# A decoder step with a 32-expert mixture: gate and up weights read with 16 neighbouring rows per partition, and the gathered tokens permuted to match

## The reference, cut to what matters

```python
def hier_moe(xn, p):                  # D_MODEL 2048, 32 experts, MOE_FF 256, float32
    t = xn.reshape(-1, D_MODEL)       # 264 tokens
    ...                               # router: a group of 8 experts, then the 2 best in it
    hg = jnp.einsum('td,edf->tef', t, p['moe_w_gate'])
    hu = jnp.einsum('td,edf->tef', t, p['moe_w_up'])
    hmid = jax.nn.silu(hg) * hu * gates[..., None]
    out = jnp.einsum('tef,efd->td', hmid, p['moe_w_down'])
```

## Time and profile before

| | us |
|---|---|
| median of three runs | 1730.24 (1726.53 to 1732.93) |
| the profiled execution, its own time | 1727.93 |
| its span in the trace | 1725.7 |
| up to the end of `xa_wo` | 1099 |
| router block and the way to the first expert matmul | 1099 to 1154 |
| experts, 16 pairs | 1154 to 1700 |
| final norm and output | 1700 to 1725.7 |

### The profile page before, as it was taken

How to read it: one execution, slowest core, us unless ns; L and a number is a source line. 1 busy time by engine, 2 the same in 40 slices (tenths; PEclk the granted TensorE clock), 3 DMA queues, 4 the chain that set the end, 5 groups by cost and what they waited for, 6 DMA issues and landing times. The chain is left out here.

```text
span 1725.7 us, 20054 instructions
## 1 busy us (share of the span) xinstructions
PE 1571.8 (91%) x7823; PEld 1132.5 (66%) x7823; DVE 675.3 (39%) x1860; ACT 287.2 (17%) x772; POOL 213.9 (12%) x305
## 2 busy tenths in 40 slices
PE   7999989989888788997999699759999999999987
PEld 5888867767677677876886388535545644554445
DVE  3536439999955731001345000332112211321123
ACT  3111101111112321000212000221211211121103
POOL 1110135665610000110000011020000000000000
PEclk9999999999989999998999899879999999999999
DMA  9644433333342566442656956309999999999981
GB/s 282 213 147 144 139 110 110 110 110 110 120 131 86 177 189 199 148 149 96 236 195 248 337 153 243 97 12 367 365 374 373 365 365 378 370 365 364 379 308 51
DMA packets 317993, 376.10 MB, mean 218 GB/s; under 512 B 24931, under 2 KB 289423, under 8 KB 309442
## 3 DMA queue, kind: packets, MB, share of 16 engines
q1 hardware_dynamic: 313242, 370.62, 64.3%
q10 hardware_dynamic: 4664, 4.28, 0.7%
HBM read 363.44 MB, written 11.54 MB: 217 GB/s over the span
## 5 line engine op out<-in xcount | busy, mean ns | idle before, releaser
L917 PE MATMUL ps<-ring,M 128*128 128x256 f32 x1024 | 247.6, 400 | 1.6 <-ACT M L930 1.6
L2342 PE MATMUL ps<-ring,M 128*64 128x512 f32 x1024 | 227.5, 597 | 14.1 <-DMA ring<-in_moe_w_up 13.4
L300 PE MATMUL ps<-X,ring 128*128 128x264 f32 x1024 | 230.1, 388 | 7.5 <-PEq L1497 6.4
L917 PEld LDWEIGHTS ps<-ring,M 128*128 128x128 f32 x1024 | 201.7, 201 | 43.2 <-issue 14.8
L300 PEld LDWEIGHTS ps<-X,ring 128*128 128x128 f32 x1024 | 195.6, 191 | 41.8 <-issue 8.1
L630 PE MATMUL ps<-X,ring 128*128 128x264 f32 x896 | 205.1, 390 | 0.0
L630 PEld LDWEIGHTS ps<-X,ring 128*128 128x128 f32 x896 | 170.8, 192 | 29.4 <-issue 0.4
L2342 PEld LDWEIGHTS ps<-ring,M 128*64 128x64 f32 x1024 | 79.7, 138 | 158.7 <-issue 157.7
L2507 DVE TENSOR_TENSOR M<-M,ps 128x256 f32<-128x256 f32 x16 | 6.7, 421 | 420.2 <-ACT M L2429 420.2
L1795 PE MATMUL ps<-X,ring 128*128 128x264 f32 x512 | 120.0, 392 | 9.4 <-PEq L1549 9.4
L2353 PE MATMUL ps<-SH 128*128 128x264 f32 x512 | 118.2, 389 | 0.7 <-ACT SH L2443 0.7
(11 more groups left out here) (431 smaller groups left out, 1569.0 us busy)
## 6 DMA issues: line engine op xcount, KB each, us to landing
SH<-in_moe_w_down SPq DMA_DIRECT2D x32, 2048.0 KB, 14.7
ring<-in_moe_w_gate SPq DMA_DIRECT2D x64, 1024.0 KB, 11.7
ring<-in_moe_w_up SPq DMA_DIRECT2D x64, 1024.0 KB, 11.9
ring<-in_w_in SPq DMA_DIRECT2D x14, 2048.0 KB, 8.5
ring<-in_xa_wk SPq DMA_DIRECT2D x8, 2048.0 KB, 9.1
ring<-in_xa_wv SPq DMA_DIRECT2D x8, 2048.0 KB, 9.0
ring<-in_w_out SPq DMA_DIRECT2D x8, 2048.0 KB, 8.4
SH<-in_cache_mem_k SPq DMA_DIRECT2D x8, 2048.0 KB, 9.7
```

The source lines that it names most:

```text
L300: mm = nc.tensor.matmul(ps[:, b, 0:T], w[:, k, o * P:(o + 1) * P], xn[:, k, :], start=(k == 0), stop=(k == KB - 1))
L917: mm = nc.tensor.matmul(ps[:, kv_bank(s), a * 256:(a + 1) * 256], memT[:, k, a * P:(a + 1) * P], w[:, k, :], start=(k == 0), stop=(k == KB ...
L2342: mm = nc.tensor.matmul(ps[64 * e:64 * e + 64, 0, :], xg[:, p % 3, k, e, :], gate_up_unit(e, half)[:, :, k % 8, :], start=(k == 0), stop=( ...
```

## The change

The rows of the gate and up weights are split as `(p k)` in place of `(k p)`: partition p gets the 16 neighbouring rows 16p to 16p + 15. A unit takes 8 of these 16, which lie behind one another in memory: a run of 8 KB for each partition in place of 8 runs of 1 KB. The bytes, the buffers and SP's order stay. The matmul's block k then holds the dimensions 16m + k for m from 0 to 127, and no longer 128k + m. So the tokens are put in that order too:

- the prompt tokens when they leave PSUM in the router: the same instructions as before read the bank with a step of 16 numbers, 16 times 32 of them, and write runs of 32 numbers;
- the 8 samples by a new way: 16 transposes in four groups into bank 3, four ScalarE copies that permute them into `xs_tok`, 16 transposes back, and a ScalarE copy into `xsT`, from which GpSimd fills the lists;
- the branch for long lists rebuilds `xn` in the new order by matmuls (it is not taken with these inputs).

```diff
+        def rows_of_expert(name, e):
+            w = I[name][0]
+            return w[e].rearrange("(p k) n -> p k n", k=KB) if isinstance(e, int) else \
+                w[bass.ds(e, 1)].rearrange("o (p k) n -> p (o k) n", k=KB)
...
                     sp.dma_start(gate_up_unit(j % 2, half)[:, w, :, :],
-                                 of_expert(name, e)[:, 8 * half:8 * half + 8, :]).then_inc(unit_loaded[j].sem, 16)
+                                 rows_of_expert(name, e)[:, 8 * half:8 * half + 8, :]).then_inc(unit_loaded[j].sem, 16)
...
         def tok_block(x, n):
-            return x[:, n % 2, 512 * (n // 2):512 * (n // 2) + 512]
+            return x[:, n % 2, :].rearrange("p (k m) -> p k m", k=KB)[:, :, 32 * (n // 2):32 * (n // 2) + 32]
+        def tok_bank(b, rows=P):
+            return ps[0:rows, b, :].rearrange("p (m k) -> p k m", k=KB)
+        xs_tok = work[0:TS, 0:2048].rearrange("p (k m) -> p k m", k=KB)
+        xsT = work[:, 3400:3528].rearrange("p (k b) -> p k b", b=TS)
...
+                for n in range(4):                                   # TensorE, ahead of its wait for chosen_ready
+                    if n:
+                        pe.wait_ge(strow_taken.sem, strow_taken.at(n))
+                    for k in range(4 * n, 4 * n + 4):
+                        mm = nc.tensor.transpose(ps[0:TS, 3, (k % 4) * P:(k % 4 + 1) * P], xn[:, k, TP:T], ident[:, :])
+                    mm.then_inc(strow_done.sem, strow_done.up())
+                pe.wait_ge(strow_taken.sem, strow_taken.at(4))
+                for k in range(KB):
+                    mm = nc.tensor.transpose(ps[:, 3, TS * k:TS * k + TS], xs_tok[:, k, :], ident[0:TS, 0:TS])
+                mm.then_inc(st_done.sem, st_done.up())
...
                 pool.wait_ge(chosen_ready.sem, chosen_ready.at(1))
+                pool.wait_ge(st_taken.sem, st_taken.at(1))
...
-                        gp.tensor_copy(xg[:, b, :, e, CAP:CAP + TS], xn[:, :, TP:T])
+                        gp.tensor_copy(xg[:, b, :, e, CAP:CAP + TS], xsT)
...
-                    nc.scalar.copy(tok_block(x_parts[0], n), ps[:, 4 + n % 4, :]).then_inc(part_ready.sem, part_ready.up())
+                    nc.scalar.copy(tok_block(x_parts[0], n), tok_bank(4 + n % 4)).then_inc(part_ready.sem, part_ready.up())
...
+                for n in range(4):                                   # ScalarE, ahead of the two exponentials
+                    act.wait_ge(strow_done.sem, strow_done.at(n + 1))
+                    nc.scalar.copy(xs_tok[:, :, 32 * n:32 * n + 32], tok_bank(3, TS)).then_inc(
+                        strow_taken.sem, strow_taken.up())
+                act.wait_ge(st_done.sem, st_done.at(1))
+                nc.scalar.copy(xsT.rearrange("p k b -> p (k b)"), ps[:, 3, 0:P]).then_inc(st_taken.sem, st_taken.up())
                 act.wait_ge(r_arg.sem, r_arg.at(1))
                 nc.scalar.activation(rt[:, 0:12], rt[:, 0:12], ACT.Exp).then_inc(r_exp.sem, r_exp.up())
```

More of the change, by code:

```diff
@@ L2046, in build @@
                                             "token_rest_ready", "logit_rows_done", "logit_rows_taken"))
+        strow_done, strow_taken, st_done, st_taken = (signal(f"router_{n}") for n in (
+            "sample_rows_transposed", "sample_rows_taken", "samples_transposed_back", "samples_taken"))
         with nc.Block() as block:
@@ L2138, in _ @@
                     first_part(n)
-                    nc.scalar.copy(tok_block(x_tok, n), ps[:, 4 + n % 4, :]).then_inc(raw_taken.sem, raw_taken.up())
+                    nc.scalar.copy(tok_block(x_tok, n), tok_bank(4 + n % 4)).then_inc(raw_taken.sem, raw_taken.up())
                 for n in range(4, 8):
                     second_part(n)
+                for n in range(4):
[4 more added lines that the diff above has]
+                nc.scalar.copy(xsT.rearrange("p k b -> p (k b)"), ps[:, 3, 0:P]).then_inc(st_taken.sem, st_taken.up())
                 act.wait_ge(r_arg.sem, r_arg.at(1))
@@ L2178, in _ @@
                         dve.wait_ge(part_ready.sem, part_ready.at(n + 1))
-                        tt(tok_block(x_tok, n), ps[:, 4 + n % 4, :], tok_block(x_parts[0], n), ALU.subtract).then_inc(
+                        tt(tok_block(x_tok, n), tok_bank(4 + n % 4), tok_block(x_parts[0], n), ALU.subtract).then_inc(
                             xtok_taken.sem, xtok_taken.up())
@@ L2254, in build @@
         g_silu, g_mid, g_midT = (A[:, 2800 + 256 * i:3056 + 256 * i] for i in range(3))
+        eye_b = H[:, 6144:6208].bitcast(BF16)
+        eye_ready, xn_done, xn_taken = (signal(f"moe_{n}") for n in (
+            "bf16_identity_ready", "tokens_block_rebuilt", "tokens_block_taken"))
         gates_te = gates_tok.rearrange("p a g j -> p a (g j)")
@@ L2275, in _ @@
                 with pe.If(crowd > CAP):
+                    pe.wait_ge(eye_ready.sem, eye_ready.at(1))
+                    for k in range(KB):
+                        if k >= 4:
+                            pe.wait_ge(xn_taken.sem, xn_taken.at(k - 3))
+                        for a in range(2):
+                            for part in range(3):
+                                mm = nc.tensor.matmul(ps[:, 4 + k % 4, a * P:(a + 1) * P],
+                                                      x_parts[part][:, a, k * P:(k + 1) * P], eye_b,
+                                                      start=(part == 0), stop=(part == 2))
+                        mm.then_inc(xn_done.sem, 1)
+                    pe.wait_ge(xn_taken.sem, xn_taken.at(KB + 1))
                     for e in range(EXPERTS):
@@ L2459, in _ @@
                 with dve.If(crowd > CAP):
+                    v.tensor_copy(eye_b, ident[:, :]).then_inc(eye_ready.sem, 1)
+                    for k in range(KB):
+                        dve.wait_ge(xn_done.sem, xn_done.at(k + 1))
+                        v.tensor_copy(xn[:, k, 0:TP], ps[:, 4 + k % 4, 0:TP]).then_inc(xn_taken.sem, 1)
+                    v.tensor_copy(xn[:, :, TP:T], xsT).then_inc(xn_taken.sem, 1)
                     for e in range(EXPERTS):
```

## The result

The changed kernel takes 1715.29 us (median of 4 runs, 1710.92 to 1718.06), the kernel before 1729.82 on the same chip (4 runs, 1726.53 to 1732.93). The ratio is 0.9914 with a 95% interval of 0.9885 to 0.9943: 14.5 us or 0.86% faster. The forecast was 1716 and "faster". Its sum is right to 1 us, yet three of its terms were mis-sized and their errors cancel, which is luck. The traces show this.

What follows compares the result with a forecast made beforehand. Weight transfers were taken to bound the experts' stage by a hair, TensorE next. 1727.93 - 15.1 (loads) + 1.5 (router) = 1714.3, or 1716 us on the median's level; range 1709 to 1730, the forecast case's own 1711 to 1719.

Steps and rivals of the forecast that it cites:

- The bound: Experts' stage: weight transfers set the pace by a hair, 33.96 us a usual pair; TensorE's 33.59 us is next.
- The rate: Gate and up loads: 8 KB runs go at 418 GB/s, cautiously 388, against 348 for 1 KB runs.
- The rivals on the memory's pitch: Gate and up loads: no faster with 8 KB runs, 1732 us (chance 0.08), or slower, 1765 us (0.05).
- The gain in the stage: Experts' stage: all 15 waits on up loads go, 13.4 us plus 1.7 of half-speed clock, 15.1 us gained.
- the wait's price: Experts' stage: TensorE's listed idle time on up loads, 13.4 us in 15 waits, 0.37 in a usual pair.
- The router: Router's last chain: the samples' new copies and transposes make it end 1.5 us later, bounds 0 and 4.
- the slack of 5.2 us: Router: ScalarE has its first exponential at 1127.91 us, VectorE wants it at 1133.13; 6.5 us of work is added.
- a round of four transposes: Router, samples' way: four transposes at 0.12 us each with 0.1 of handover, 0.6 us a round, three rounds.
- The permuted reads: Router: PSUM reads with a step of 16 numbers cost nothing; the rival that they cost, 1724 us, chance 0.13.
- The two rules: Router's PSUM reads: skill rules against non-contiguous access; one gives 0.35 us per 512-column read, some 4 us on the chain.
- The price for small packets: Loads: the skill's fixed 3 cycles a packet lose 8% at 1 KB and 1% at 8 KB, 398 against 430 GB/s.
- The end: Last scatter to the end of the span: no change, 0 us.

Runs made afterwards that it cites:

- the two kernels with a light gather: The kernel before and the changed kernel, each without two of the gather's three bf16 parts: 1724.68 and 1676.23 us, beside 1729.43 for before.
- second trace: The changed kernel run once more, nothing altered, on the same chip as the others, for its trace: 1710.64 us, ratio 0.9898.
- the changed kernel's third trace: The changed kernel unaltered, run beside the kernel without the samples' way on the same chip: 1711.61 us, ratio 0.9909.

## Why the prediction was right

- **The bound.** "The weights set the pace, by a hair" and the next limit, TensorE's own work, hold: the two kernels with a light gather show both sides, and 2 KB and 8 KB loads meet the same limit to 0.01 us.
- **The rate.** Taken as 418 GB/s with 388 as the cautious end. Measured 406 to 442 for 8 KB runs and 388 for 2 KB. The rivals on the memory's pitch fall: half of every 16 KB is read at full rate.
- **The gain in the stage, forecast 15.1, measured 18.3.** The term that was mis-sized is the wait's price. I took the idle time that the waits list (13.4 us) and a pair of 33.59 us, TensorE's busy time. Measured start to start, that is up to the next group, the scatter (line 2353 before, with the row below), the two halves of gate_up take 1264.83 - 1250.40 = 14.43 us before and 1236.35 - 1222.52 = 13.83 after. The wait thus cost 0.60 us where the list says 0.37; the matmuls run into one another, and the modelled end of the last one ahead of a gap, and the refilling after it, count as busy; this is my reading of why, and no run tests it. The difference itself is there in all 15 pairs, 0.22 us each, 3.3 us in all. The last pair has it too: its gate_up took 20.48 us start to start and takes 13.86, that is 6.6 for the 4.70 + 1.69 of the sum. Added up start to start, the 15 pairs before lose 18.4 us, which is all that the stage gained.

```profile
1264.83 7.39 PE L2353 MATMUL ps<-SH 128*128 128x264 f32 x32
```

- **The router, forecast 1.5, measured 2.6 to 3.3** in the traces with the early clock (57.58 before; 60.19, 60.46 and 60.85 after). The step was right: ScalarE's queue, the slack of 5.2 us, VectorE late by the rest. ScalarE's new part took 7.75 us where I had 6.5. The term at fault is a round of four transposes, put at 0.6 with handover: it took 1.1. The four take 1.02 us behind each wait, as TensorE's clock was at half again after 4.8 us of idleness (0.50 from 1131 to 1139 us); 0.12 each came from a row at full clock, and the first four, ahead of the idleness at a clock of 1.00, take 0.60 (second trace). This accounts for VectorE's chain, which ends 2.3 to 2.5 us later than before's (42.88 to 43.03 us after the last addition of `xa_wo`, before's 40.57). The other 0.3 to 0.8 us arise between there and the first expert matmul; no run separates them. The first trace has the late clock on top.
- **The permuted reads, forecast 0.** Right: the casts from PSUM take 602 ns on the mean, as before, and the kernel without the samples' way shows no loss. The two rules that the prediction took from the Trainium skill, "SBUF — State Buffer", section "Door 1: The DMA port swizzle", and "Vector Engine (DVE) Microarchitecture Reference", section "Measured stream behaviour on trn2", do not carry over to ScalarE and VectorE reading PSUM with a step of 16 numbers: 602 ns and 688 ns against 602 and 686. The price for small packets by the Trainium skill, "DMA: Bandwidth & Descriptors", section "Why small descriptors are slow", was 8% for 1 KB; the traces show 348 against 418 GB/s, 17%.
- **The end, forecast 0, measured 0.6 to 1.5** in the ten traces without waits on loads (33.6 to 34.5 us, before's 33.01). This was not foreseen. The last 48 transposes, behind TensorE's wait for the final norm, take 7.04, 7.04 and 6.96 us in the three kernels with the old 1 KB loads and 7.74 to 8.30 in the ten others. They are not all of it: what follows them takes 5.6 to 6.7 us without regard to the loads, so that of the three kernels with old loads two end after 33.01 and 33.06 us, and the one with the light gather after 33.87. The granted clock falls to half in both kernels: in the kernel before the stretches of 2 us from 1712 us on have 0.68, 0.50 and 0.97, in the changed kernel's third trace those from 1694 us on have 0.74, 0.50, 0.50, 0.55 and 1.00. Why this should depend on a wait or its absence 20 us earlier is not settled, and no run was made for it.

In sum, with the changed kernel's third trace: -18.4 + 2.6 + 0.9 = -14.9, beside 14.5 measured; the forecast had -15.1 + 1.5 = -13.6. The bound, the place of the gain and the place of the price were right; that the total came within 1 us is the luck of 3.3 us too little gain against 2.0 us too little price.

## What to carry to other kernels

Where two limits lie within a few per cent, price a change by the nearer limit: here a 20% faster load was worth 1% of the time, and 2 KB runs gave the loads' whole gain in their stage (what token order they need, and its price, no run here shows). Read a wait between matmuls from start to start of the groups around it, with a group that has no wait beside it; the idle time in the list was 0.22 us too low in each of the 15 places here. A chain of small steps between two engines that is "hidden" has to be summed with the clock that the idle engine will really have.

## What the runs showed of the hardware that was not expected

- The rate of a load followed the length of its runs, and in the cases measured not the share of memory that they leave out: 348 GB/s at 1 KB, 388 at 2 KB (in two kernels, reading a quarter of each 8 KB and without gaps), 406 to 442 at 8 KB.
- A single 1 MB load of 8 KB runs does not land sooner: from issue to landing the gate loads take 11.8 us in the median where they took 11.7, the up loads 14.1 for 11.9, while the down loads take 11.7 for 14.7. SP is no longer held back while it issues (0.4 us for an up load at 1263.56 us, where one at 1258.11 us took 6.44 before), so that the same queueing is counted from an earlier issue. The rate has to be read from stretches, not from this column.
- After some 5 us without work TensorE's clock was at half, and four small transposes took 1.02 us in place of 0.60. The moment at which it rises again differs between executions of one program, worth 0.95 us in the router here.
